# Latent attention in sets of four heads with 32-row scores, and the first two weight pieces together

## The chip, the cores and the metric

The kernel runs on one core of a Trainium2 chip. The metric is the device time in microseconds of one execution; the median of three runs of the kernel before is 1009.23 us (1008.88 to 1009.68). A matmul on this core multiplies a stationary operand (up to 128 rows by 128 columns, loaded by its own instruction) with a moving one of up to 512 columns and writes to a PSUM bank. There are eight banks of 128 partitions x 512 float32.

## The reference, cut to what matters

The model is a stack of two equal layers on x of 512 tokens by 1024 channels, float32, with a last RMSNorm. Each layer normalises x, projects it with w_in to three mixer branches and their gates, runs the branches (A: banded attention with sinks, B: gated linear attention, C: latent attention), projects each back, merges them by sigmoid gates, multiplies by w_out and adds x. The change touches branch C and the order of the first projections:

```
q_c = (rmsnorm(cq, cq_g) @ w_uq).reshape(B, S, 8, 64 + 32)        # q_nope, q_rope per head
kv  = (rmsnorm(ckv, ckv_g) @ w_ukv).reshape(B, S, 8, 64 + 64)     # k_nope, v per head
k_rope = rope(kr)                                                 # 32 numbers, shared by the heads
for each block of 128 queries:
    s = (q_nope @ k_nope.T + q_rope @ k_rope.T) * 96 ** -0.5
    s = where(key_chunk <= query_chunk, s, -1e30)                 # chunks of 64 tokens
    p = softmax(s);  y = p @ v
yc = y * silu(gc);  zc = yc @ w_oc
```

So query block 0 sees up to 128 keys, block 3 up to 512.

## The kernel before

**Pieces and quarters.** All weights come as 77 pieces of 128 x 1024 a layer. SP loads a piece into one of three buffers (`raw`). ScalarE rounds it to the high part `w_hi` (L793), VectorE makes the low part `w_lo` (L1095), and TensorE multiplies each tile three times (high x high, low x high, high x low; L569). TensorE takes a piece in four quarters; a quarter of a gate piece is six matmuls of 512 columns, and a piece's output lands in one of three ring banks, `ring0` to `ring2`. A buffer of `w_hi` is free when its piece is done, so ScalarE splits piece p + 3 right behind the last quarter of p, and VectorE its low part behind the second quarter of p + 1.

**What sets the order.** `make_schedule` writes one list of steps. Every engine walks through the same list in order and does its own part of each step, with semaphores between them. An engine that waits therefore holds back everything of its own that stands later in the list. `quarters(n)` takes n quarters of the fill, the gate pieces of branch C (53 to 64, 48 quarters), and adds a tanh (ScalarE, L951) after each piece and, for the first four, a silu (VectorE).

**The latent projections.** Piece 46 (`PUKV`) has eight outputs of 512 columns, four of v (even) and four of k (odd); pieces 47 and 48 (`PUQ`) have three each, the first two of them the rotary parts of q. An output of k or q holds two heads of 64 rows: ScalarE copies the upper 64 partitions (L865, L871), VectorE the lower ones (L1470, L1490), so that `k_c` and `q_c` hold every head in partitions 0 to 63, with the rotary parts in 64 to 95, brought by DMA through DRAM from ScalarE's queue.

**The latent attention.** There are 32 steps a layer, one for a head and a query block. `score_c` is one matmul of 96 rows by 128 columns against n = 128 to 512 keys into bank `nat[i % 2]` (L740). VectorE masks (L1350), takes the row maximum (L1352) and scales it (L1355); ScalarE makes the exponentials with their sum (L1014); VectorE takes the reciprocal (L1373) and multiplies (L1375, step `divide`). `turn` transposes the probabilities in blocks of 128 into the one bank `nat[2]` (L750), ScalarE copies them out (L1026), and `value_c` multiplies them with v for two heads at a time into `nat[3]`, 64 columns each (L777). Behind each eighth step `gate_branch` multiplies by the gate (L1114); `y_hi` and `y_lo` split the result. The steps are staggered: a turn is two steps behind its score, and one quarter stands between two steps.

**The start.** x comes as eight tiles. SP sends tile 0, half of piece 0, tile 1, its other half, tiles 2 to 7, then pieces 1 and 2. ScalarE and VectorE split the tiles as they come, TensorE does piece 0 tile by tile, then pieces 1 and 2. Then comes the sum of squares (`rms`, L641) and piece 3.

Of the kernel before, what the change touches and what calls it, by code (L numbers as in the profile page):

```python
# [66 lines left out]

def by_act(r):

    return sum(first_output(p) + o < r for p in (PUKV, PUQ, PUQ + 1) for o in range(outputs_of(p)) if act_reads(p, o))  # L70


def shared(p, o):

    return (p == PUKV and o % 2 == 1) or (p, o) == (PUQ, 2) or p == PUQ + 1


def act_reads(p, o):

    return p == PUKV or shared(p, o)  # L80


def by_dve(r):

    return r - sum(first_output(PUKV) + o < r for o in range(0, 8, 2))


def emptied_by(r):

    for p in (PUKV, PUQ, PUQ + 1):  # L90
        o = r - first_output(p)
        if 0 <= o < outputs_of(p):
            return not act_reads(p, o) or shared(p, o), act_reads(p, o)
    return True, False
# [17 lines left out]
def make_schedule():  # L112
# [85 lines left out]
    def quarters(n):  # L198

        for _ in range(min(n, len(fill))):  # L200
# [3 lines left out]
            if q % 4 == 3 and g is not None:  # L204
                b, j = g
                todo.append(("tanh", 12 * b + j))
                if 1 <= j <= BR:
                    todo.append(("silu", BR * b + j - 1))

# [26 lines left out]
    nc_ = TT * C_HEADS  # L236
    quarters(10)
    for i in range(nc_ + 3):
        if 2 <= i < nc_ + 2:
            todo.append(("turn", na + i - 2))  # L240
        if 1 <= i <= nc_:
            todo.append(("divide", na + i - 1))
        if i < nc_:
            todo.append(("score_c", i))
        if i >= 4 and i % 2 == 0:
            todo.append(("value_c", (i - 4) // 2))
        quarters(1)
        y, h = divmod(i - 3 + 1, C_HEADS)
        if y >= 1 and h < 2:
            todo.append((("y_hi", "y_lo")[h], TT + y - 1))  # L250
# [34 lines left out]
def build_hybrid_trunk(nc, x_t, pieces, params, alpha, tables, consts, final_g, out_t, k_rope_dram, q_rope_dram):  # L285
    with ExitStack() as ctx:
# [3 lines left out]
        def sig(name, per_layer, before=0):  # L290
# [39 lines left out]
        prob, prob_t = [work[:, i, :] for i in range(3)], [work[:, 3 + i, :] for i in range(4)]  # L330

# [3 lines left out]
        k_c = bank_g[:, :].rearrange("p (h n) -> p h n", h=C_HEADS)  # L335
# [5 lines left out]
        q_c = bank_a[:, 0:4096].rearrange("p (h n) -> p h n", h=C_HEADS)  # L341
# [20 lines left out]
        nat = [ctx.enter_context(nc.psum_tensor(f"nat{i}", [P, S], F32)) for i in range(4)]  # L362
        aux = ctx.enter_context(nc.psum_tensor("aux", [P, S], F32))
        turn_bank, o_bank = nat[2], nat[3]
# [7 lines left out]
        first_loaded, first_hi, first_lo = sig("first_loaded", 0), sig("first_hi", 0), sig("first_lo", 0)  # L372
# [23 lines left out]
        k_rope_saved, k_rope_placed = sig("k_rope_saved", 16), sig("k_rope_placed", 16)  # L396
        q_rope_saved, q_rope_placed = sig("q_rope_saved", 32), sig("q_rope_placed", 32)
# [12 lines left out]
        masked = sig("masked", A_KV + TT * C_HEADS)  # L410
        top_set = sig("top_set", 2 * TT * A_KV + TT * C_HEADS)
        neg_top_set, exp_done = sig("neg_top_set", n_steps), sig("exp_done", n_steps)
        turn_done, turn_out, value_done = (sig("turn_done", n_steps), sig("turn_out", n_steps),
                                           sig("value_done", TT * A_KV + TT * C_HEADS // 2))
        denom_set, divided = sig("denom_set", 2 * TT * A_KV + TT * C_HEADS), sig("divided", n_steps)
# [14 lines left out]
        def attention_of(step):  # L430

            if step < TT * A_KV:
                return "a", step // A_KV, step % A_KV, step // A_KV
            c = step - TT * A_KV
            return "c", c // C_HEADS, c % C_HEADS, TT + c // C_HEADS
# [7 lines left out]
        def _(sp):  # L443
            for j in range(KT):
                sp.dma_start(xt[:, j, :], x_t[:, j, :]).then_inc(x_loaded[j].sem, 16)  # L445
                if j == 0:
                    sp.dma_start(raw[:, 0, 0:512], pieces[0, :, 0:512]).then_inc(first_loaded.sem, 16)
                elif j == 1:
                    sp.dma_start(raw[:, 0, 512:1024], pieces[0, :, 512:1024]).then_inc(raw_loaded[0].sem, 16)
            for i in range(1, RAW):  # L450
                sp.dma_start(raw[:, i, :], pieces[i]).then_inc(raw_loaded[i].sem, 16)
# [4 lines left out]
            for n in range(RAW, DEPTH * PIECES):  # L456
                layer, p = divmod(n - RAW, PIECES)
                if p in (PQA[1] + 3, PQA[3] + 3):
# [3 lines left out]
                    for hh in range(GROUP):  # L462
                        for half in range(2):
                            sp.dma_start(q_a[64 * pair + 32 * half:64 * pair + 32 * half + 32, hh, :],
                                         work[32 * hh:32 * hh + 32, 4 + half, :]).then_inc(q_placed.sem, 16)
                sp.wait_ge(lo_split.sem, n - RAW + 1)
# [19 lines left out]
        def _(pe):  # L486
            def project(layer, quarter):
# [4 lines left out]
                if (layer, p, part) == (0, 0, 0):  # L492
                    pe.wait_ge(first_lo.sem, 1)
                elif part == 0 or (layer, p, part) == (0, 0, 2):
# [80 lines left out]
            def last_pieces():  # L575

                layer = DEPTH - 1
                for m in range(4):
# [9 lines left out]
                    for k in range(KT):  # L588
# [4 lines left out]
                        if (m, k) == (2, 5):  # L593
                            pe.wait_ge(aux_free.sem, aux_free.at(DEPTH, 0))
# [19 lines left out]

            def aux_bank(layer, u):
# [10 lines left out]
            for layer in range(DEPTH):  # L626
                u = 0
                for name, i in SCHEDULE:
                    if name == "quarter" and layer == DEPTH - 1 and i // 4 >= PIECES - 2:
                        if i == 4 * (PIECES - 2):  # L630
                            last_pieces()
                        continue
                    if name == "quarter":
                        project(layer, i)
                        continue
                    if (name, i) == ("rms", 0):

                        aux_bank(layer, u)
                        pe.wait_ge(setup_loaded.sem, SETUP)
# [91 lines left out]
                    elif name == "score_c":  # L731
                        qt, h = divmod(i, C_HEADS)
# [883 lines left out]
```

## Time and profile before

| | |
|---|---|
| median of three runs | 1009.23 us |
| the profiled execution | 1008.85 us, its span 1007.0 us |
| TensorE matmuls | busy 992.1 us (99%), 5168 instructions |
| VectorE | busy 624.7 us (62%) |
| ScalarE | busy 427.3 us (42%) |
| chain that ended last | TensorE 91%, ScalarE 3%, VectorE 3% |
| granted TensorE clock | 0.997 of full |
| latent attention in the chain | scores L740 3%, transposes L750 3%, values L777 2% |

Matmuls are pipelined: a record of a matmul is longer than its distance to the next one. What a matmul costs is read from the chain of waits, whose pieces stand end to end. An fp32 matmul (scores, values) shows as two instructions, a transpose as one, and each of the three products of L569 as one.

### The profile page before, as it was taken

What the parts mean: (1) busy time and instruction counts of PE and PEld (TensorE: products, weight loads), DVE (VectorE), ACT (ScalarE), POOL (GpSimd) and SP (SyncE); (2) the same over time, 40 slices, a digit from 0 to 9 for tenths busy, and PEclk for the clock granted to TensorE, in tenths of its full rate; (3) what the DMA queues carried; (4) which work ended last, traced back from release to release, by engine and by line L of the source; (5) the groups of instructions that cost most, each with busy time, mean ns of one, the idle gap of its engine ahead of it and who ended that gap; (6) DMA issues with size and microseconds to landing.
All of it is one profiled execution on the core that took longest, in us unless ns stands there. A gap on an engine that the chain in (4) does not pass through costs nothing.

```text
span 1007.0 us, 13335 instructions
## 1 busy us (share of the span) xinstructions
PE 992.1 (99%) x5168; PEld 792.8 (79%) x5168; DVE 624.7 (62%) x1142; ACT 427.3 (42%) x804; POOL 1.6 (0%) x6
## 2 busy tenths in 40 slices
PE   8999999999999999999999999999999999999996
PEld 6878878887777877788888887888877787767885
DVE  7746448546647576666556655584575667765844
ACT  6343335425542355533435333542354424554323
POOL 0000000000000000000000000000000000000000
PEclk9999999999999999999999999999999999999998
DMA  7323311322135211022223332122221522111212
GB/s 261 124 70 132 125 64 65 123 86 84 64 105 146 84 63 62 37 75 101 95 77 118 105 119 84 67 101 105 84 79 69 154 102 80 43 49 58 96 51 84
DMA packets 29952, 92.93 MB, mean 92 GB/s; under 512 B 3825, under 2 KB 6129, under 8 KB 29762
## 3 DMA queue, kind: packets, MB, share of 16 engines
q1 hardware_dynamic: 27362, 88.07, 24.7%
q10 hardware_dynamic: 2528, 4.02, 1.6%
q8 instruction: 41, 0.67, 0.3%
q14 instruction: 21, 0.17, 0.1%
HBM read 86.24 MB, written 3.28 MB: 89 GB/s over the span
## 4 chain that ended last, share of the span: by engine, by line
PE 91%; ACT 3%; DVE 3%; issue 1%; DMA 1%; SPq 0%; POOLq 0%; POOL 0%; ACTq 0%; DVEq 0%
PE ring L569 72%; PE nat L569 5%; PE nat L740 3%; PE nat L750 3%; PE nat L777 2%; ACT w_hi L793 1%; PE nat L763 1%; PE nat L703 1%; PE nat L726 1%; DVE w_lo L1095 1%; DMA raw<-pieces 1%; PE nat L691 0%; ACT gates L1042 0%; SPq L445 0%; PE aux L665 0%
## 5 line engine op out<-in xcount | busy, mean ns | idle before, releaser
L569 PE MATMUL ring<-act_hi,w_hi 128*128 128x512 f32 x848 | 348.8, 411 | 1.1 <-DVE w_lo L1095 0.9
L569 PE MATMUL ring<-act_hi,w_lo 128*128 128x512 f32 x848 | 331.1, 390 | 0.0
L569 PE MATMUL ring<-act_lo,w_hi 128*128 128x512 f32 x848 | 330.9, 390 | 0.0
L793 ACT ACTIVATE w_hi<-raw 128x1024 fp32r<-128x1024 f32 x153 | 161.5, 1057 | 340.2 <-PE ring L569 308.7
L1095 DVE TENSOR_TENSOR w_lo<-raw,w_hi 128x1024 fp32r<-128x1024 f32 x153 | 186.4, 1219 | 54.2 <-ACT w_hi L793 54.1
L569 PEld LDWEIGHTS ring<-act_hi,w_hi 128*128 128x128 f32 x848 | 159.3, 188 | 45.8 <-issue 11.8
L569 PEld LDWEIGHTS ring<-act_hi,w_lo 128*128 128x128 f32 x848 | 159.2, 188 | 34.4
L569 PEld LDWEIGHTS ring<-act_lo,w_hi 128*128 128x128 f32 x848 | 159.5, 188 | 32.6 <-issue 1.9
L1402 DVE SCALAR_TENSOR_TENSOR gates<-ring,rstd 128x512 f32<-128x512 f32 x72 | 49.7, 690 | 115.8 <-PE ring L569 115.2
L569 PE MATMUL ring<-y_hi,w_hi 128*128 128x512 f32 x192 | 74.8, 390 | 0.4 <-DVE bank_a L1490 0.4
L569 PE MATMUL ring<-y_hi,w_lo 128*128 128x512 f32 x192 | 74.7, 389 | 0.0
L569 PE MATMUL ring<-y_lo,w_hi 128*128 128x512 f32 x192 | 74.7, 389 | 0.0
L1014 ACT ACTIVATE work<-nat,neg_top 128x128 f32<-128x128 f32 (+3 forms) x64 | 33.8, 528 | 67.4 <-DVE neg_top L1355 67.2
L1026 ACT ACTIVATE work<-nat 128x512 f32<-128x512 f32 (+3 forms) x80 | 37.1, 463 | 32.7 <-PE nat L750 32.3
L569 PE MATMUL nat<-w_hi,act_hi 128*128 128x512 f32 (+1 forms) x128 | 49.1, 383 | 0.5 <-DVE w_lo L1095 0.5
L569 PE MATMUL nat<-w_lo,act_hi 128*128 128x512 f32 (+1 forms) x128 | 47.8, 374 | 0.0
L569 PE MATMUL nat<-w_hi,act_lo 128*128 128x512 f32 (+1 forms) x128 | 47.8, 373 | 0.0
L740 PE MATMUL nat<-bank_g,bank_a 96*128 96x128 f32 (+3 forms) x128 | 45.1, 433 | 0.0
L951 ACT ACTIVATE gates<-gates 128x512 f32<-128x512 f32 x72 | 43.6, 618 | 0.0
L569 PEld LDWEIGHTS ring<-y_hi,w_hi 128*128 128x128 f32 x192 | 36.0, 188 | 8.7 <-issue 1.2
L569 PEld LDWEIGHTS ring<-y_hi,w_lo 128*128 128x128 f32 x192 | 36.0, 188 | 7.5
L569 PEld LDWEIGHTS ring<-y_lo,w_hi 128*128 128x128 f32 x192 | 36.0, 188 | 7.4
(193 smaller groups left out, 1041.3 us busy)
## 6 DMA issues: line engine op xcount, KB each, us to landing
raw<-pieces SPq DMA_DIRECT2D x153, 512.0 KB, 3.5
xt<-x_t SPq DMA_DIRECT2D x8, 256.0 KB, 6.0
bank_a<-work SPq DMA_DIRECT2D x32, 64.0 KB, 2.0
out_t<-gates SPq DMA_DIRECT2D x7, 256.0 KB, 2.3
rope<-tables SPq DMA_DIRECT2D x1, 1024.0 KB
bank_g<-k_rope_dram ACTq DMA_DIRECT2D x2, 512.0 KB, 4.2
q_rope_dram<-work ACTq DMA_DIRECT2D x4, 256.0 KB, 2.2
bank_a<-q_rope_dram ACTq DMA_DIRECT2D x4, 256.0 KB, 6.2
```

Source lines behind the costliest of these rows:

```text
L569: mm = pe.matmul(dst, stationary, moving, start=start and i == 0, stop=stop and i == 2)
L703: mm = pe.matmul(nat[2 * pair + h][:, cs], state[half, c, pair, :], q_b[half, pair, cs], start=True, stop=True)
L726: mm = pe.matmul(nat[g][c * 64:c * 64 + 64, hh * P + skip:(hh + 1) * P], q_a[rows, hh, q0:q0 + CHUNK], k_a[rows, k0:q0 + CHUNK], start=Tru ...
L740: mm = pe.matmul(nat[i % 2][:, 0:n], q_c[0:C_DH, h, qt * P:(qt + 1) * P], k_c[0:C_DH, h, 0:n], start=True, stop=True)
L750: mm = pe.transpose(turn_bank[:, b * P:(b + 1) * P], prob[i % 3][:, b * P:(b + 1) * P], ident)
L777: mm = pe.matmul(o_t[r * 64:r * 64 + 64, f, :], v_c[:, b, h * C_V:(h + 1) * C_V], prob_t[(step + r) % 4][:, b * P:(b + 1) * P], start=b == ...
L793: nc.scalar.activation(w_hi[:, n % HL, :], raw[:, n % RAW, :], ACT.Copy).then_inc(hi_split.sem, 1)
L951: nc.scalar.activation(gates[:, j if j >= 4 else 8 + j, :], gates[:, j, :], ACT.Tanh).then_inc(gate_tanh.sem, 1)
L1014: nc.scalar.activation(prob[step % 3][:, 0:n], nat[i % 2][:, 0:n], ACT.Exp, scale=C_SCALE, bias=neg_top[:, step % 2, 0:1], accum_out=sums[ ...
L1026: nc.scalar.activation(prob_t[i % 4][:, 0:n], turn_bank[:, 0:n], ACT.Copy).then_inc(turn_out.sem, 1)
L1095: nc.vector.tensor_tensor(w_lo[:, n % HL, :], raw[:, n % RAW, :], w_hi[:, n % HL, :].bitcast(F32), ALU.subtract).then_inc(lo_split.sem, 1)
L1402: nc.vector.scalar_tensor_tensor(gates[:, j, :], res, 0.5, rstd[:, :], ALU.mult, ALU.mult).then_inc(proj_free.sem, 1)
```

## The change

Four things change.

1. **Scores in sets of four heads.** The rows of k and q are laid out so that head a of a set (a = 0 to 3) sits in partitions 32a to 32a + 31, in three parts: two halves of the 64 unrotated rows (`q_n`, `k_n`) and the rotary 32 (`q_r`, `k_r`). A score is three matmuls of 32 rows that add up in one bank; the four heads go to the four banks `nat[0]` to `nat[3]`. There are 8 sets a layer, 12 matmuls each. Transposes go back into the bank that the head's scores came from, and the values of a set are one group. The values' output moves to bank `aux`. VectorE masks four heads and reduces two at a time.
2. **Projections.** An output of v, and each of q, is emptied by ScalarE alone, one of k by VectorE alone, 128 partitions at a time. The rotary parts of k go by 4 DMAs of SP, ahead of the load of piece 52, those of q by 16, ahead of the load of piece 55.
3. **The order of the steps.** A set is: score, values of the set before, a quarter, divide, a quarter, `y_hi` of a finished query block, 1, 1, 2 or 3 quarters (by query block), `y_lo`, transposes, a quarter.
4. **The start.** The first halves of pieces 0 and 1 come behind tiles 0 and 1, their second halves behind tiles 3 and 4; TensorE does both pieces together, into two ring banks.

TensorE in the first layer, third query block (384 keys), before. L750 are transposes, L740 a score, L777 values, L569 the fill:

```order
1526 L750 MATMUL nat<-con,work 128x128 x3
1527 L740 MATMUL nat<-bank_g,bank_a 128x384
1528 L777 MATMUL nat<-work,bank_a 64x128 x4
1529 L569 MATMUL ring<-act_hi,w_hi 128x512
1530 L569 MATMUL ring<-act_lo,w_hi 128x512
```

The same place now, the sixth set (L782 transposes, L775 scores, L818 values, L575 the fill):

```order
1506 L782 MATMUL nat<-con,work 128x128 x12
1507 L575 MATMUL ring<-act_hi,w_hi 128x512
1508 L575 MATMUL ring<-act_lo,w_hi 128x512
1509 L575 MATMUL ring<-act_hi,w_lo 128x512
1510 L575 MATMUL ring<-act_hi,w_hi 128x512
1511 L575 MATMUL ring<-act_lo,w_hi 128x512
1512 L575 MATMUL ring<-act_hi,w_lo 128x512
1513 L775 MATMUL nat<-bank_g,bank_a 128x384 x12
1514 L818 MATMUL aux<-work,bank_a 64x128 x7
```

One transpose group, score and value group stand for four heads, and the score comes a quarter behind the transposes of the set before it, whose copies it waits for.

ScalarE in the same query block, before. L1014 is an exponential, L1026 a copy of transposes, L793 a weight split, L951 a tanh:

```order
472 L1014 ACTIVATE work,sums<-nat,neg_top 128x384
473 L793 ACTIVATE w_hi<-raw 128x1024
474 L951 ACTIVATE gates<-gates 128x512
475 L1026 ACTIVATE work<-nat 128x384
476 L1014 ACTIVATE work,sums<-nat,neg_top 128x384
```

ScalarE now, the fifth set and the start of the sixth (L1037 exponentials, L1058 `y_hi`, L834 weight split, L971 tanh, L1050 copies):

```order
386 L1037 ACTIVATE work,sums<-nat,neg_top 128x384 x4
387 L1058 ACTIVATE y_hi<-y_pre 128x4x128
388 L834 ACTIVATE w_hi<-raw 128x1024
389 L971 ACTIVATE gates<-gates 128x512
390 L1050 ACTIVATE work<-nat 128x384 x3
391 L1050 ACTIVATE bank_a<-nat 128x384
392 L1037 ACTIVATE work,sums<-nat,neg_top 128x384 x4
```

Four copies in a row now stand behind the split and the tanh of a piece that ends right before the transposes.

SP at the start, before (x_t is x, pieces the weights):

```order
1 L445 DMA xt<-x_t 128x512
2 L447 DMA raw<-pieces 128x512
3 L445 DMA xt<-x_t 128x512
4 L449 DMA raw<-pieces 128x512
5 L445 DMA xt<-x_t 128x512 x6
6 L451 DMA raw<-pieces 128x1024 x2
```

SP at the start now:

```order
1 L442 DMA xt<-x_t 128x512
2 L444 DMA raw<-pieces 128x512
3 L442 DMA xt<-x_t 128x512
4 L444 DMA raw<-pieces 128x512
5 L442 DMA xt<-x_t 128x512 x2
6 L446 DMA raw<-pieces 128x512
7 L442 DMA xt<-x_t 128x512
8 L446 DMA raw<-pieces 128x512
9 L442 DMA xt<-x_t 128x512 x3
10 L447 DMA raw<-pieces 128x1024
```

Piece 1 moved ahead of the last tiles of x, in two halves.

The core of the diff:

```diff
+    for y in range(2 * TT):
+        qt = y // 2
+        todo.append(("score_c", y))
+        if y > 0:
+            todo.append(("value_c", y - 1))
         quarters(1)
+        todo.append(("divide_c", y))
+        quarters(1)
+        if y > 0 and y % 2 == 0:
+            todo.append(("y_hi", TT + qt - 1))
+        quarters((1, 1, 2, 3)[qt])
+        if y > 0 and y % 2 == 0:
+            todo.append(("y_lo", TT + qt - 1))
+        todo.append(("turn_c", y))
+        quarters(1)
...
-        mm = pe.matmul(nat[i % 2][:, 0:n], q_c[0:C_DH, h, qt * P:(qt + 1) * P],
-                       k_c[0:C_DH, h, 0:n], start=True, stop=True)
+        pe.wait_ge(turn_out.sem, turn_out.at(layer, NA + 4 * i))
+        for part in range(3):
+            for a in range(4):
+                rows = slice(32 * a, 32 * a + 32)
+                q, k = ((q_n[rows, g, part, ts], k_n[rows, g, part, 0:n]) if part < 2 else
+                        (q_r[rows, g, ts], k_r[rows, 0:n]))
+                mm = pe.matmul(nat[a][:, 0:n], q, k, start=part == 0, stop=part == 2)
...
+    elif name == "turn_c":                                   # ScalarE
+        act.wait_ge(value_done.sem, value_done.at(layer, NA + i))
+        for a in range(4):
+            act.wait_ge(turn_done.sem, turn_done.at(layer, NA + 4 * i + a + 1))
+            nc.scalar.activation(prob_ct[a][:, 0:n], nat[a][:, 0:n], ACT.Copy).then_inc(turn_out.sem, 1)
...
+    for k in range(2):                                       # VectorE, divide_c
+        h = 4 * g + 2 * k
+        dve.wait_ge(exp_done.sem, exp_done.at(layer, NA + 4 * i + 2 * k + 2))
+        nc.vector.reciprocal(recip[:, h:h + 2], sums[:, qt, h:h + 2]).then_inc(denom_set.sem, 1)
...
+    elif p == PUQ + 5:                                       # SP
+        sp.wait_ge(rope_out.sem, rope_out.at(layer, 10))
+        for g, half, a in ((g, half, a) for g in range(2) for half in range(2) for a in range(GROUP)):
+            sp.dma_start(q_r[32 * a + 16 * half:32 * a + 16 * half + 16, g, :],
+                         work[64 * g + 16 * a:64 * g + 16 * a + 16, 2 * half, :]).then_inc(q_rope_placed.sem, 16)
...
-    for o in ((2,) if p == PUQ else range(3)):               # VectorE
-        nc.vector.tensor_copy(q_c[0:64, h, :], ring[(first_output(p) + o) % 3][0:64, :])
...
+def first_pieces():                                          # TensorE
+    jobs = [(p, k) for p in range(2) for k in range(2)] + [(p, k) for k in range(2, KT) for p in range(2)]
```

## Rows read from the trace of the kernel before

**Rows 1.** The page: engine busy time, and shares of the chain.

```profile
PE 992.1 (99%) x5168; PEld 792.8 (79%) x5168; DVE 624.7 (62%) x1142; ACT 427.3 (42%) x804; POOL 1.6 (0%) x6
PE 91%; ACT 3%; DVE 3%; issue 1%; DMA 1%; SPq 0%; POOLq 0%; POOL 0%; ACTq 0%; DVEq 0%
```

**Rows 2.** Chain of waits, first layer's latent attention: start us, us, what.

```profile
343.26 0.22 PE nat L740 x2
...
409.38 0.44 PE nat L750 x4
409.82 0.86 PE nat L740 x2
410.68 1.38 PE ring L569 x6
...
413.35 1.02 PE nat L777 x16
414.38 1.58 PE ring L569 x6
...
431.14 0.89 PE ring L569 x3
```

**Rows 3.** Timeline of TensorE: start us, us, instruction; one banded score group.

```profile
238.38 1.10 PE L726 MATMUL nat<-bank_a 64*64 64x128 f32 x32
```

**Rows 4.** Chain of waits, first layer's gated linear attention.

```profile
130.89 0.60 PE nat L691 x16
...
139.87 1.04 PE nat L703 x16
```

**Rows 5.** Groups of weight loads by line: busy us, mean ns of one.

```profile
L740 PEld LDWEIGHTS nat<-bank_g,bank_a 96*128 96x128 f32 x128 | 19.7, 191 | 1.4
...
L691 PEld LDWEIGHTS nat<-bank_g 64*64 64x64 f32 x128 | 3.4, 132 | 2.8 <-issue 2.8
```

**Rows 6.** Groups by line and form on ScalarE and VectorE.

```profile
L1014 ACT ACTIVATION_READ_ACCUMULATOR work<-nat,neg_top 128x1 f32 x64 | 12.4, 193 | 0.0
...
L1352 DVE TENSOR_REDUCE top<-nat 128x1 f32<-128x512 f32 x16 | 11.1, 691 | 0.5
...
L1014 ACT ACTIVATE work<-nat,neg_top 128x512 f32<-128x512 f32 x16 | 11.0, 688 | 18.2 <-DVE neg_top L1355 18.2
...
L1026 ACT ACTIVATE work<-nat 128x384 f32<-128x384 f32 x16 | 7.8, 488 | 4.4 <-PE nat L750 4.0
L1375 DVE TENSOR_SCALAR work<-work,recip 128x512 f32<-128x512 f32 x16 | 7.8, 486 | 0.6
```

**Rows 7.** Chain of waits at the third step of the latent attention.

```profile
345.08 1.39 PE ring L569 x6
...
348.14 0.17 ACT work L1026
...
348.44 0.30 PE nat L750
```

**Rows 8.** Timeline of TensorE, latent projections and first output projection.

```profile
305.26 0.39 PE L569 MATMUL ring<-lat_hi,w_lo 128*128 128x512 f32 x1
305.79 0.47 PE L569 MATMUL ring<-lat_hi,w_hi 128*128 128x512 f32 x1
...
307.02 0.39 PE L569 MATMUL ring<-lat_hi,w_lo 128*128 128x512 f32 x1
307.63 0.47 PE L569 MATMUL ring<-y_hi,w_hi 128*128 128x512 f32 x1 [0.22 <-DVE bank_a L1490]
```

**Rows 9.** Timeline at the start, TensorE and VectorE.

```profile
15.24 0.50 PE L569 MATMUL ring<-act_hi,w_hi 128*128 128x512 f32 x1 [0.91 <-DVE w_lo L1095]
...
24.33 2.28 DVE L1095 TENSOR_TENSOR w_lo<-raw,w_hi 128x1024 fp32r<-128x1024 f32 x2
...
26.30 1.02 PE L641 MATMUL aux<-merged,ones_r 128*128 128x512 f32 x2
```

**Rows 10.** SP's queue: rotary parts of the banded queries.

```profile
73.19 6.05 SPq L464 DMA_DIRECT2D bank_a<-work  x8
```

More of the change, by code:

```diff
@@ L65, in first_output, with act_reads @@
     return sum(outputs_of(q) for q in range(p))
+def act_reads(p, o):
+    return (p == PUKV and o % 2 == 0) or (p, o) == (PUQ, 2) or p == PUQ + 1
 def by_act(r):
     return sum(first_output(p) + o < r for p in (PUKV, PUQ, PUQ + 1) for o in range(outputs_of(p)) if act_reads(p, o))
[L73 to L80, printed above, removed]
 def by_dve(r):
-    return r - sum(first_output(PUKV) + o < r for o in range(0, 8, 2))
+    return r - by_act(r)
 def emptied_by(r):
[L90 to L94, printed above, removed]
+    by_scalar = by_act(r + 1) > by_act(r)
+    return not by_scalar, by_scalar
 def signals_before(p):
@@ L206, in quarters @@
                 todo.append(("tanh", 12 * b + j))
-                if 1 <= j <= BR:
+                if 1 <= j <= BR and (b, j) != (2, BR):
                     todo.append(("silu", BR * b + j - 1))
+                if (b, j) == (2, BR - 1):
+                    todo.append(("silu", BR * b + j))
     fill = [4 * p + q for p in [*range(PO[0], PO[0] + 4), *range(PG[1], PG[1] + 12)] for q in range(4)]
@@ L235, in make_schedule @@
     fill = [4 * p + q for p in range(PG[2], PG[2] + 12) for q in range(4)]
[L236 to L246, printed above, removed]
-        quarters(1)
-        y, h = divmod(i - 3 + 1, C_HEADS)
-        if y >= 1 and h < 2:
-            todo.append((("y_hi", "y_lo")[h], TT + y - 1))
+    quarters(8)
+    for y in range(2 * TT):
[3 more added lines that the diff above has]
+            todo.append(("value_c", y - 1))
+        quarters(1)
+        todo.append(("divide_c", y))
[7 more added lines that the diff above has]
+        quarters(1)
+    todo.append(("value_c", 2 * TT - 1))
+    quarters(1)
+    todo.append(("y_hi", 2 * TT - 1))
     quarters(len(fill) - 1)
@@ L330, in build_hybrid_trunk @@
         prob, prob_t = [work[:, i, :] for i in range(3)], [work[:, 3 + i, :] for i in range(4)]
+        prob_c, prob_ct = [work[:, i, :] for i in range(4)], [*(work[:, 4 + i, :] for i in range(3)), bank_a[:, 3072:3584]]
         k_dec = bank_g[:, 0:1024].rearrange("p (t n) -> p t n", t=TT)
@@ L632, in _ @@
                         continue
+                    if name == "quarter" and layer == 0 and i // 4 < 2:
+                        if i == 0:
+                            first_pieces()
+                        continue
                     if name == "quarter":
@@ L748, in _ @@
                             pe.wait_ge(turn_out.sem, turn_out.at(layer, i))
-                        for b in range(GROUP if kind == "a" else qt + 1):
+                        for b in range(GROUP):
                             mm = pe.transpose(turn_bank[:, b * P:(b + 1) * P], prob[i % 3][:, b * P:(b + 1) * P], ident)
```

339 lines of the change are left out of this document (170 added, 169 removed).

## The prediction, made before the changed kernel ran

> **What bounds the kernel now.** The page comes first: TensorE is busy for 992.1 of 1007.0 us and makes up 91% of the chain that ended last [rows 1]. So an edit counts by what it does to TensorE's stream, and by the few gaps in it. Then the chain of waits inside the first layer's latent attention, from the first score to the last value group, 343.26 to 431.14 us [rows 2]: it is an unbroken row of TensorE pieces, a score matmul being two instructions (0.22 us at 128 keys, 0.86 at 512, so 0.43 and 0.65 between), a transpose 0.11, a value group of 16 instructions 1.02, a fill quarter of six matmuls 1.38, or 1.58 behind a value group. ScalarE and VectorE are hidden there but for one gap near 348 us [rows 7]. The second layer repeats it. Last come the start [rows 9] and the latent projections [rows 8], where TensorE does wait.
>
> **Scores.** Before, 32 matmuls a layer, 8 for each query block: 8 x (0.22 + 0.43 + 0.65 + 0.86) = 17.3 us. After, a set of four heads is 12 matmuls of 32 rows, 24 instructions, and there are 8 sets. An instruction streams as long as before, so a set costs 24 half-prices over the number of row groups that really work side by side. No row shows four row groups. The nearest by kind is the banded score L726: 32 instructions of 64 rows x 64 columns, four tiles at a time (two row groups by two column groups), took 1.10 us where one behind the other they would take 32 x 0.108 = 3.5: less some 0.2 for the change of mode, that is four at a time [rows 3]. I take four: 6 half-prices, 0.65, 1.30, 1.94 and 2.59 us.
>
> The weight loads may set a floor. The state readout L703 loads 128 columns for every 64-column stream: 16 instructions took 1.04 us, less 0.17 of entry 0.054 each [rows 4]. At that rate 24 loads need 1.30 us, more than the 0.65 of a 128-key set. In the other direction, a 128-column load lasts 191 ns against 132 for 64 columns [rows 5], so a column costs 0.9 ns and 128 of them about 0.11 us; two row groups must then have loaded side by side in L703, and four could give 0.65 us per set. I take 1.30, the row of the same width. Four sets of 128 keys in all make 2.6 us between the ends.
>
> Sets of one layer: 2 x (1.30 + 1.30 + 1.94 + 2.59) = 14.3 us, 3.0 less than before, **6.0 for both layers**. The ends: 8.6 if loads run four abreast; below, if row groups overlap less, the rivals.
>
> **Changes of mode.** A value group of 16 costs 1.02 - 16 x 0.054 = 0.16 us to enter, and the quarter behind it is 0.20 longer than one behind a score [rows 2]. Before: 16 groups a layer, 5.8 us. After: 8 entries into the 32-row mode at 0.17 (L691: 0.60 - 16 x 0.027 [rows 4]), 8 into the value mode, 9 ways back: 1.36 + 1.28 + 1.80 = 4.4. **Saved 1.3 a layer, 2.6 in all.** If the way between the two small modes were free or double, that is 1.1 us for each layer to either side. Transposes and values stay at 80 x 0.11 and 160 x 0.054.
>
> **Waits inside a set.** All four banks now hold one set from score to transpose, so between score and transposes stand only three to five quarters and the last value group. The longest chain, 512 keys: two reductions over a pair (about twice 0.69 each [rows 6]; the first pair is ready at 1.8 us behind the score, the second at 3.2), four exponentials at some 0.78 with the accumulator read (to 4.9), reciprocals and multiplications of 0.49 (to 6.3). Cover: five quarters and a value group, 8.5 us. At 384 keys 5.5 against 6.7; at 128 keys 3.7 against 4.3. VectorE's gate evacuation (0.69) and one silu stand ahead of the reductions, and are over as the first scores end. For the third set two silus stand there, the second behind its tanh; then the pairs are ready at 5.7 to 6.9 us after the quarter, and the transposes, one head after another, start at 6.4. Hidden, with little to spare.
>
> One wait isn't hidden. In the fifth set (384 keys) the transposes come right behind a piece's last quarter. On ScalarE that quarter's weight split and tanh then stand ahead of the four copies out of the banks; the next score waits for all four. The chain at 346 us shows how long: quarter over at 346.48, tanh through at 348.14 [rows 7]. So the copies start 1.75 us after the transposes begin, four of 0.49 (0.43 apart, since they overlap) end at 3.6; TensorE has 1.3 of transposes and one quarter, 2.7. **0.95 us lost a layer**; before lost about 0.4 near 348. Net +1.1 for both. With shorter copies this is 0; if the same happened in the third and sixth sets too, +4.
>
> **Latent projections.** k_c and q_c were emptied half by ScalarE, half by VectorE, each with 64 partitions and about the time that 128 take. Now one engine takes one output. VectorE's q copies stood behind six rotary operations and a weight split; TensorE waited for them: 305.26 + 0.23 to 305.79, and 307.02 + 0.23 to 307.63 [rows 8], 0.68 us. They go, since ScalarE is idle there. The earlier gaps hang on the first v copy and on the rotary multiplications and stay. **1.4 us for both layers** (0 to 3). The rotary parts go through 16 DMAs of SP ahead of piece 55's load. Eight of that kind took 6.05 us to issue [rows 10], so 16 about 12 us, from 310 to 322 us. The load is then some 6 us late, but its split is due only near 329 and the first score near 340.
>
> **Start.** TensorE waits 0.91 us ahead of piece 1, which starts at 15.24; pieces 1 and 2 end at 26.30 [rows 9]. Three pieces are 72 x 0.227 = 16.3 us and could start at about 8.2: 24.6. With both pieces fed by each tile of x, a tile gives 1.36 us of work and the splits take 0.7 to 1.4, so TensorE stays fed. But piece 3 needs its low part, which VectorE starts at 24.33 behind the squares and has at 25.5. TensorE would want it at about 25.1 after the mean square; before, the mean square started at 26.30 and piece 3 at about 27.1. **1.6 us** (0.5 if the tiles moved back in the queue arrive late, 2.2 if VectorE gets ahead too).
>
> **Sum.** 6.0 + 2.6 - 1.1 + 1.4 + 1.6 = 10.5 us. The profiled execution took 1008.85 us, so 998.35; the median of the runs is 0.4 higher: **998.7 us**. About 0.2% (2 us) is what a measurement of this kernel can tell from no change.
>
> **Rivals.**
> A. Row groups overlap threefold only, by a shared path into or out of the array. For it: in L726 only two row groups ran at a time. Against it: there the factor was whole. Price: sets of 1.30, 1.73, 2.59 and 3.45 us, 18.1 a layer instead of 14.3, +7.7: 1006.4 us. Beside this: the Trainium skill, "TensorE: Matmul & The Clock Gate", in "Measured speedup vs the span model", gives 3.07-fold for four row tiles of K=32 and N=512; by that figure the time would be an estimated 1006 us. No row here shows four row groups, and the L726 row points the other way.
> B. Row groups go in pairs, since each stream of four writes all 128 partitions of its own bank. This is the slower case. Its place is every set. For it: L703, the only row with 128-column outputs from two row groups, took 0.87 us net for sixteen streams of 0.054, which is also what no overlap at all would give [rows 4]. Against it: L691 and L726. Price at two abreast: 12 half-prices, 1.30, 2.59, 3.89, 5.18: 25.9 a layer, 11.6 more than my sum: 998.7 + 23 = 1022 us. It decides below about 2.6 abreast; there the sets eat up the other gains. With no overlap, 24 half-prices, 51.8 a layer: 1074 us.
> C. The sets' chain is too long for its cover, as four banks leave no second set in flight. For it: the chain at 346 us shows ScalarE's queue reaching TensorE. Against it: the covers worked out above. At 1 us in each of the first four sets of a layer: +8, 1006.7 us.
> D. Loads go four abreast and the copies of the fifth set are in time: 998.7 - 2.6 - 1.9 = 994.2 us.
>
> **How the numbers follow.** My forecast 0.55, D 0.15, A 0.1, C 0.07, B 0.1 with both its forms, other 0.03. The range 994 to 1007 takes in D, A and C and leaves out B. Faster holds the forecast, D, A and most of C: 0.84. Within 0.2%: 0.05, from the edge of A and C. Slower: 0.11.
>
> **What would show it.** In the new chain, 24 score instructions at 512 keys in about 2.6 us (3.5 speaks for A, 5.2 for B), at 128 keys 1.3 (0.65 for D). A wait for ScalarE's copies of about 1 us ahead of the sixth set's score, in both layers, and none of size at the other sets. No VectorE wait near 305 and 307. The start of piece 3 near 25.5 us. Matmul starts within a set that stand one stream apart instead of four at once would make the forecast wrong.

## The result and the profile after

The changed kernel took 994.08 us (median of 4 runs, 993.81 to 994.21) against 1009.45 us before (1008.88 to 1009.75): ratio 0.9849, 95% interval 0.9837 to 0.9861, 15.4 us faster. The forecast was 998.7 us, with 994.0 to 1007.0 as the range. The direction was right, and so was the mechanism, four row groups abreast. The time came out almost exactly where rival D put it (994.2 us). D's ground, weight loads four abreast, is what the trace shows; that the number agrees so closely is in part luck, as the part on the prediction works out.

The page after, engine busy time [rows 1]:

```profile
PE 978.3 (99%) x5424; PEld 791.6 (80%) x5424; DVE 600.6 (61%) x991; ACT 417.8 (42%) x797; POOL 1.6 (0%) x6
```

TensorE is as full as before and has 13.8 us less to do; it still sets the time. The chain of waits of the changed kernel through the first layer's latent attention (start us, us, what) answers to [rows 2]:

```profile
338.04 0.88 PE nat L775 x24
...
343.25 0.44 PE nat L782 x4
343.69 1.38 PE ring L575 x6
...
345.95 0.59 PE aux L818 x8
346.54 4.33 PE ring L575 x18
...
352.70 1.51 PE nat L775 x24
...
372.63 1.02 PE aux L818 x16
373.65 5.68 PE ring L575 x24
...
379.42 0.69 ACT w_hi L834
...
380.38 0.31 ACT gates L971
...
380.90 1.23 ACT work L1050 x3
382.13 0.39 ACT bank_a L1050
...
394.61 2.79 PE nat L775 x24
...
405.91 1.75 PE nat L782 x16
...
411.83 1.90 PE aux L818 x32
...
425.78 2.26 PE ring L575 x9
```

Every L775 piece is one set of four heads: 24 instructions in 0.88, 1.51, 2.15 to 2.22 and 2.79 us for 128, 256, 384 and 512 keys. Less 0.23 of entry that is 0.65, 1.28, 1.92 to 1.99 and 2.56: six times the half of a matmul before (0.108, 0.216, 0.323, 0.43), at every length. Four row groups really run abreast, and so do their weight loads. A group of values (L818) costs 0.16 beside its matmuls, and the quarters behind one 0.19 more (4.33 against 3 x 1.38). Transposes (L782) cost 0.11 each and next to nothing at their borders: a quarter behind them takes 1.38 to 1.40, where six matmuls in an unbroken stretch take 6 x 0.227 = 1.36. The values of the last set end at 425.78.

The one wait is where it was forecast: behind the fifth set's transposes ScalarE has a weight split and a gate ahead of the four copies, and the sixth set's scores wait for the last copy. The timeline of TensorE there (the row holds 20 of the set's 24 instructions):

```profile
382.56 1.90 PE L775 MATMUL nat<-bank_g,bank_a 32*128 32x384 f32 x20 [0.55 <-ACT bank_a L1050]
```

In the latent projections the two VectorE waits of [rows 8] are gone; the chain is one row of TensorE from 292.93 us on, with a gap of 0.11 us in it:

```profile
292.93 8.01 PE ring L575 x33
300.93 0.11 issue
301.04 11.16 PE ring L575 x48
```

At the start, piece 3 comes at 26.08 us, still behind VectorE's low part. Piece 3 was forecast for 25.5; the low part begins at 24.88, 0.55 us later than in [rows 9], where I had left it:

```profile
24.88 2.28 DVE L1118 TENSOR_TENSOR w_lo<-raw,w_hi 128x1024 fp32r<-128x1024 f32 x2
...
26.08 0.46 PE L575 MATMUL nat<-w_hi,act_hi 128*128 128x432 f32 x1 [0.74 <-DVE w_lo L1118]
```

The kernel before has one more wait for VectorE's low part a little later, which is gone now:

```profile
42.11 0.47 PE L569 MATMUL nat<-w_hi,act_hi 128*128 128x432 f32 x1 [0.26 <-DVE w_lo L1095]
```

SP's sixteen rotary transfers took 10.00 us to issue, from 308.65 us, and nothing waited for them, as forecast from [rows 10]:

```profile
308.65 10.00 SPq L472 DMA_DIRECT2D bank_a<-work  x16
```

The span fell by 15.0 us (1007.0 to 992.0). By stages: TensorE reaches the first expansion 1.56 us earlier; from there to the next branch each layer is 0.83 shorter (15.52 to 14.69); the stage of the latent attention, from there to the first matmul of the branch's own output projection, 5.7 shorter in the first layer (129.02 to 123.3) and about the same in the second; about 0.4 is left over at the end. 1.56 + 2 x 0.83 + 2 x 5.7 + 0.4 = 15.0. The stage begins and ends with these matmuls now (before, 307.63 [rows 8] and 436.65):

```profile
305.24 0.39 PE L575 MATMUL ring<-y_hi,w_hi 128*128 128x512 f32 x1
...
428.56 0.39 PE L575 MATMUL ring<-y_hi,w_hi 128*128 128x512 f32 x1
```

### The profile page after: what moved, and what is told of

It is laid out like the page before. It is cut to its first block, busy times and chain, and to the rows that moved or that the text cites. A ratio compares the mean times of both kernels' runs of the same rounds, so it can differ in the third digit from the quotient of the medians.

```text
span 992.0 us, 13563 instructions
## 1 busy us (share of the span) xinstructions
PE 978.3 (99%) x5424; PEld 791.6 (80%) x5424; DVE 600.6 (61%) x991; ACT 417.8 (42%) x797; POOL 1.6 (0%) x6
## 4 chain that ended last, share of the span: by engine, by line
PE 92%; ACT 3%; DVE 2%; issue 1%; DMA 1%; SPq 1%; POOLq 0%; POOL 0%; ACTq 0%; DVEq 0%
PE ring L575 72%; PE nat L575 7%; PE nat L775 3%; PE aux L818 2%; PE nat L782 1%; PE aux L804 1%; PE nat L790 1%; PE nat L732 1%; PE nat L755 1%; DMA raw<-pieces 1%; ACT w_hi L834 1%; PE nat L720 0%; DVE w_lo L1118 0%; SPq L442 0%; ACT gates L1065 0%
## 5 line engine op out<-in xcount | busy, mean ns | idle before, releaser
L575 PE MATMUL ring<-act_hi,w_hi 128*128 128x512 f32 x832 | 333.5, 401 | 0.0
L575 PE MATMUL ring<-act_hi,w_lo 128*128 128x512 f32 x832 | 325.1, 391 | 0.0
L575 PE MATMUL ring<-act_lo,w_hi 128*128 128x512 f32 x832 | 324.7, 390 | 0.0
L834 ACT ACTIVATE w_hi<-raw 128x1024 fp32r<-128x1024 f32 x152 | 160.5, 1058 | 352.2 <-PE ring L575 320.4
L575 PEld LDWEIGHTS ring<-act_hi,w_hi 128*128 128x128 f32 x832 | 156.3, 188 | 37.8 <-issue 7.2
L575 PEld LDWEIGHTS ring<-act_hi,w_lo 128*128 128x128 f32 x832 | 156.2, 188 | 33.6
L575 PEld LDWEIGHTS ring<-act_lo,w_hi 128*128 128x128 f32 x832 | 156.5, 188 | 30.1
L575 PE MATMUL ring<-y_hi,w_lo 128*128 128x512 f32 x192 | 74.8, 389 | 0.0
L575 PE MATMUL ring<-y_hi,w_hi 128*128 128x512 f32 x192 | 74.8, 389 | 0.0
L575 PE MATMUL ring<-y_lo,w_hi 128*128 128x512 f32 x192 | 74.8, 389 | 0.0
L575 PE MATMUL nat<-w_hi,act_hi 128*128 128x512 f32 (+1 forms) x128 | 48.7, 381 | 1.0 <-DVE w_lo L1118 1.0
L1037 ACT ACTIVATE work<-nat,neg_top 128x128 f32<-128x128 f32 (+3 forms) x64 | 32.9, 526 | 38.7 <-DVE neg_top L1380 38.7
L575 PE MATMUL nat<-w_lo,act_hi 128*128 128x512 f32 (+1 forms) x128 | 47.9, 374 | 0.0
L575 PE MATMUL nat<-w_hi,act_lo 128*128 128x512 f32 (+1 forms) x128 | 47.8, 374 | 0.0
L971 ACT ACTIVATE gates<-gates 128x512 f32<-128x512 f32 x72 | 43.6, 618 | 1.7 <-DVE gates L1431 1.6
L575 PEld LDWEIGHTS ring<-y_hi,w_lo 128*128 128x128 f32 x192 | 36.1, 188 | 7.5
L575 PEld LDWEIGHTS ring<-y_lo,w_hi 128*128 128x128 f32 x192 | 36.1, 188 | 7.5
L575 PEld LDWEIGHTS ring<-y_hi,w_hi 128*128 128x128 f32 x192 | 36.1, 188 | 7.4
L775 PE MATMUL nat<-bank_g,bank_a 32*128 32x128 f32 (+3 forms) x384 | 30.4, 446 | 1.1 <-ACT bank_a L1050 1.1
L1481 DVE SCALAR_TENSOR_TENSOR gates<-gates,ring 128x512 f32<-128x512 f32 x32 | 22.0, 687 | 14.8 <-PE ring L575 14.8
```

The source lines that it names most:

```text
L575: mm = pe.matmul(dst, stationary, moving, start=start and i == 0, stop=stop and i == 2)
L775: mm = pe.matmul(nat[a][:, 0:n], q, k, start=part == 0, stop=part == 2)
L834: nc.scalar.activation(w_hi[:, n % HL, :], raw[:, n % RAW, :], ACT.Copy).then_inc(hi_split.sem, 1)
L971: nc.scalar.activation(gates[:, j if j >= 4 else 8 + j, :], gates[:, j, :], ACT.Tanh).then_inc(gate_tanh.sem, 1)
L1037: nc.scalar.activation(prob_c[a][:, 0:n], nat[a][:, 0:n], ACT.Exp, scale=C_SCALE, bias=neg_top[:, i % 2, a:a + 1], accum_out=sums[:, qt, 4 ...
L1481: nc.vector.scalar_tensor_tensor(merged[:, j, :] if b == 0 else tile, tile, 1.0, z, ALU.add, ALU.mult).then_inc(proj_free.sem, 1)
```

## The experiments

Medians are of runs beside runs of the kernel before on the same chip; the ratio is to that kernel, with its 95% interval. The changed kernel was run again as the measure: 994.24 us (993.95 to 994.67), 0.9850 (0.9836 to 0.9863). The runs stand on three chips, on which the kernel before took 1009.39, 1009.27 and 1009.29 us, so their times can be set beside each other.

> The changed kernel unchanged, as the measure for the others on the same chip: 994.1 us, ratio to before 0.985. Every theory expects that.

**Two small parts undone.** First the start of before:

```
-            def first_pieces():  (both pieces, tile by tile)
+            project(layer, i) for pieces 0 and 1, piece 0 loaded in halves, piece 1 behind the tiles of x
```

> The start of before with the rest of the change. In the two traces TensorE comes to the second latent projection's expansion 1.56 us earlier after the change (290.55 against 292.11 us). If that is all that the new start brings, and nothing later takes it back, this kernel is 1.4 to 1.8 us slower than the changed one (about 995.7). If TensorE would later have stood at a transfer anyway, the difference is under 0.5 us.

Measured 995.97 us (995.54 to 996.03), 0.9866 (0.9853 to 0.9880): 1.7 us slower than the changed kernel. The intervals of the ratios overlap, the runs themselves do not. The new start is worth what its stage shows, and nothing takes it back. Both waits of the old start, 0.9 us at piece 1 and 0.26 near 42 us, are back in its trace.

Then the emptying of the query accumulators:

```
-    return (p == PUKV and o % 2 == 0) or (p, o) == (PUQ, 2) or p == PUQ + 1
+    return p == PUKV and o % 2 == 0          (VectorE copies the four others)
```

> VectorE alone empties the query accumulators that the change gave to ScalarE (one of the second query piece's outputs and the three of the last). In before TensorE stood there four times, near 305.3 to 307.6 us, and the stretch from the first expansion to the next branch fell from 15.52 to 14.69 us per layer, 0.83. Theory: the sharing of the emptying between two engines is what removed these waits, so here 0.5 to 0.8 us per layer come back, 1.0 to 1.6 us in all (about 995.4). Rival: the shorter stretch comes from two accumulators and their copies of 64 rows that are gone altogether, and who empties the rest is of no account: under 0.3 us.

Measured 995.45 us, 0.9861 (0.9847 to 0.9874), 1.2 us slower. The intervals of the two kernels overlap, so the trace has to carry it. Its chain of waits:

```profile
303.02 0.61 DVE bank_a L1515
303.63 0.04 issue
303.67 1.65 PE ring L575 x6
```

VectorE's rotary operations and its copy are back in the chain ahead of TensorE. From the first expansion to the first score this kernel takes 45.84 us (292.52 to 338.36) and the changed one 45.09 (292.79 to 337.88): 0.75 per layer. The sharing is what removed the waits.

**The price of a border.** The values in two groups with a quarter between:

```
-            todo.append(("value_c", y - 1))
+            todo.append(("value_h", y - 1))      first half
         quarters(1)
+            todo.append(("value_c", y - 1))      second half
```

> The values of each set stand in two groups with a quarter of a projection between them, instead of in one; the matmuls are the same. Theory: a way into the values' tiles and back out of them has a price of its own, about 0.16 us in (a group of 8 values takes 0.59 us, of 16 1.02, of 24 1.46, of 32 1.90) and 0.19 us back (three quarters take 4.33 us behind such a group, 3 x 1.38 = 4.14 elsewhere). Seven more groups in each layer make 7 x 0.35 = 2.5 us, about 5 us in all (999). Rival: the price belongs to something else, as the first use of a copied matrix, and the number of groups is of no account: under 1 us.

Measured 999.25 us, 0.9904 (0.9888 to 0.9921), 5.0 us slower, as forecast. The chain shows each half-group with its own entry and its own long quarter:

```profile
345.69 0.37 PE aux L823 x4
346.06 1.60 PE ring L578 x6
347.66 0.37 PE aux L823 x4
348.03 2.95 PE ring L578 x12
```

A group of 4 takes 0.37, that is 0.16 + 4 x 0.054, and the quarter behind it 1.60 where 1.39 is usual. 5.0 us over 14 groups (the halves of the last set have no quarter between them) is 0.36 for each: the border price is real and additive.

**The wait at the fifth set.** One quarter moved:

```
-        quarters((1, 1, 2, 3)[qt])
+        quarters((1, 1, 1, 1, 3, 2, 2, 3)[y])
```

> One quarter of a projection is moved from before the transposes of the fifth set to before those of the seventh or eighth (1, 1, 1, 1, 3, 2, 2, 3 quarters at that place instead of 1, 1, 1, 1, 2, 2, 3, 3), so that no piece of 128 columns ends just before a set's transposes. In the changed kernel TensorE stands 0.53 us at the fifth set, since ScalarE splits a weight piece (1.06 us) and takes a gate (0.61 us) before it copies the four transposed matrices. Theory: the order of these on ScalarE is the cause, and the wait goes: 0.4 to 0.6 us per layer, about 1.0 us in all (993.1). Rival: the wait moves to the seventh or eighth set, where a piece then ends at the same place and a set has four blocks: no difference, or up to 1 us slower.

Measured 993.03 us, 0.9838 (0.9824 to 0.9851), and 992.75, 0.9834 (0.9820 to 0.9847), in a second measurement on another chip:

> The kernel with the moved quarter once more, as the measure for the wide sets on the same chip: 993.0 us.

The chain has no ScalarE in it any more, and nothing new stands at the later sets:

```profile
373.36 7.03 PE ring L575 x30
380.39 1.31 PE nat L782 x12
381.70 1.39 PE ring L575 x6
383.08 2.15 PE nat L775 x24
```

From the first score to the last value it is 87.14 us, against 87.74 in the changed kernel: 0.6 per layer. Each difference in time is within what the intervals allow, but both runs and the trace agree.

**The cover of the chain.** In the sets of 384 and 512 keys one quarter between scores and transposes, instead of four and five:

```
         todo.append(("divide_c", y))
-        quarters(1)
+        quarters((1, 1, 0, 0)[qt])
...
-        quarters((1, 1, 2, 3)[qt])
+        quarters((1, 1, 0, 0)[qt])
```

> In the sets of 384 and 512 keys only one quarter of a projection stands between a set's scores (and the values of the set before) and its transposes, instead of four and five; the quarters left over stand behind the last set. In the changed kernel the chain from the end of the scores to the last multiplication takes 5.6 us at 384 keys (384.78 to about 390.4) and 5.9 us at 512 (411.83 to about 417.7). With one quarter the last head's transposes would come 2.3 to 3.0 us after the scores at 384 keys and 4.4 to 4.8 us at 512 before any wait (1.02 or 1.46 us of values at 384, 1.46 or 1.90 at 512, 0.19 + 1.38 of the quarter, three of the four transposes of 0.33 or 0.44 each). Theory: TensorE stands for the rest, and nothing gives it back: about 2.1, 1.6, 1.5 and 1.1 us, 6.3 per layer, 12.6 in all (1007; 1003 to 1010). That is the price of the chain where its cover is gone. Rival: the chain is short since its engines were late for other work only, and shrinks with the quarters: under 4 us.

Measured 1005.91 us, 0.9967 (0.9955 to 0.9979), 11.7 us slower; forecast 12.6. The transposes of the four sets end 1.7, 1.2, 1.7 and 1.3 us later than without a wait, 5.9 a layer where 6.3 was worked out. Only part of this shows as idle time of TensorE, since the transposes of a group also come further apart (us in total, times, longest):

```profile
PE nat L782 <- DVE work L1404: 9.5, 12, 1.5
```

So the chain that rival C feared is about as long as worked out, and only the fill hides it. In the changed kernel it is hidden at all eight sets. The eighth set, on VectorE and then ScalarE:

```profile
412.06 0.27 DVE L1373 MEMSET nat<- 64x256 f32 x1 [2.29 <-PE nat L775]
...
416.85 0.88 DVE L1404 TENSOR_SCALAR work<-work,recip 128x512 f32<-128x512 f32 x2
```

```profile
413.84 0.69 ACT L1037 ACTIVATE work<-nat,neg_top 128x512 f32<-128x512 f32 x1 [3.12 <-DVE neg_top L1380]
```

The scores end at 411.83, the last multiplication at 417.73 (5.9 us), and the transposes begin at 420.76.

**How four row groups come to run abreast.** Only the order of the twelve matmuls of a set was changed, in three ways. Two heads in turn:

```
-                        for part in range(3):
-                            for a in range(4):
+                        for part, a in [(part, a) for pair in ((0, 1), (2, 3)) for part in range(3) for a in pair]:
```

> The same 24 instructions of a score set with only two heads in turn: heads 0 and 1 first, then 2 and 3, so that two row groups are abreast. Theory: the time of a set goes by its stream: 12 prices of half a matmul and 0.23 us of entry instead of 6, so 1.5, 2.8, 4.1 and 5.4 us for a set of 128, 256, 384 and 512 keys instead of 0.88, 1.51, 2.2 and 2.79: 2 x (0.65 + 1.29 + 1.94 + 2.58) = 12.9 us more per layer, 25.9 in all (1020). Rival: weight loads go one after another, whatever the row group, and matmuls of 128 keys are bound by them: then the sets of 128 and 256 keys grow by less, and the sum is under 22 us.

Measured 1004.19 us, 0.9949 (0.9930 to 0.9969): 10.0 us slower, not 26. Head by head:

```
-                        for part in range(3):
-                            for a in range(4):
+                        for a in range(4):
+                            for part in range(3):
```

> The same 24 instructions of a score set, but the three matmuls of one head (one group of 32 rows, one bank) stand one behind the other instead of one of each head in turn. Theory 1: TensorE starts instructions in their order, and only neighbours of different row groups run beside each other. Then a set has hardly more than one or two abreast: up to 24 prices of half a matmul (0.108, 0.216, 0.323, 0.43 us at 128, 256, 384, 512 keys) instead of 6, and 18 more of them per set are 2 x 18 x (0.108 + 0.216 + 0.323 + 0.43) = 39 us per layer, 78 us in all; with one neighbour abreast at each change of the head (24 less 3 x 1) 66 us. Theory 2: each row group has a queue of its own, deep enough for six instructions, and they are drained beside each other: no difference.

Measured 1025.01 us, 1.0156 (1.0135 to 1.0176): 30.8 us slower, neither 0 nor 66 to 78. Both my theories of it were wrong. In pairs the theory was wrong on the size; the sum that its rival allowed (under 22 us) holds, but not its ground, since the sets of 512 keys took 3.75 us and not 5.4. The sets of pairs took 1.20, 2.04, 2.90 to 2.97 and 3.75 us, the head by head ones 1.85, 3.11, 4.39 to 4.46 and 5.67. Less entry, 512 keys are 8.2 and 12.6 half-prices. What happened is seen when a 512-key set is cut into stretches of 0.432 us, one half-price each; the count behind "PE busy" is of the matmul instructions that run in the stretch, some of them counted in two. Two heads in turn:

```profile
397.47:397.90 0.43, 0.43 (x2) 0.29 (x4) 1.00 0.72 257
397.90:398.33 0.43, 0.43 (x4) 0.19 (x2) 1.00 0.95 371
398.33:398.77 0.44, 0.44 (x6) 0.31 (x6) 1.00 1.04 428
398.77:399.20 0.43, 0.43 (x8) 0.31 (x4) 1.00 0.39 153
...
400.06:400.49 0.43, 0.43 (x6) 0.19 (x2) 1.00 0.00 0
400.49:400.93 0.44, 0.44 (x4) 0.00 (x0) 1.00 0.00 0
```

Two half-prices with one pair alone, then both pairs together, then the second pair alone: 2 + 6 = 8. Head by head the count climbs by one in a stretch:

```profile
403.86:404.29 0.43, 0.43 (x1) 0.29 (x2) 1.00 0.50 76
404.29:404.72 0.43, 0.43 (x2) 0.18 (x1) 1.00 0.72 295
404.72:405.16 0.44, 0.44 (x3) 0.29 (x3) 1.00 1.06 438
```

In the changed kernel it is 4 and then 8 at once:

```profile
394.38:394.81 0.43, 0.43 (x4) 0.31 (x8) 1.00 0.74 200
394.81:395.24 0.43, 0.43 (x8) 0.20 (x4) 1.00 1.01 410
```

Both odd results follow if a row group takes four half-instructions, one that runs and three behind it, before it holds up what follows for other row groups. A head has six. In pairs the fifth and sixth of heads 0 and 1 get in after one and two half-prices, so heads 2 and 3 start at two and end at 8. Head by head, each starts two later than the one before: 6 + 3 x 2 = 12. Since this was made to fit two numbers, it was put to a third order:

```
+                        for part, a in [(part, a) for parts in ((0, 1), (2,)) for a in range(4) for part in parts]:
```

> The order of a score set's 24 instructions between the changed kernel's and the head by head one: both matmuls of the unrotated rows of head 0, then of head 1, 2 and 3, and then the rotated rows' matmul of each head. The two runs with other orders gave 8 half-matmul prices for two heads in turn (3.75 us at 512 keys, less 0.23 of entry, by 0.43) and 12.6 for head by head (5.67), where neighbours alone abreast would give 12 and over 20. In both, a row group that comes later begins two half-prices after the six instructions of the one before it. Theory: a row group takes up to four instructions ahead (one that runs and three that stand behind it), and only the fifth holds back all that follow, on whatever row group. Then four of each row group go in at once here, and a set takes 6 half-prices as in the changed kernel: 2.79 us at 512 keys, 994.2 in all (within 1 us). Rival: what counts is how far apart two row groups' first instructions stand (here 4 instead of 2 places), or the instructions ahead in all, some 8: then a set takes 8 to 9 half-prices, 3.7 us at 512 keys, about 1004.

Measured 994.43 us, 0.9850 (0.9837 to 0.9864), the same as the changed kernel, with sets of 2.81 us at 512 keys. The rival, a limit on the instructions ahead in all, would have given some 1004. Four per row group is thus borne out: with three, this order would take 9 half-prices, and with five the head by head order would take 9 as well, since head 1 would start after one. I also worked the orders through with a bound on all instructions ahead together in place of one for each row group, and no number fits: six give 12 head by head, but 11 in pairs, and the 13 that this third order would need give 7 in pairs and 8 head by head. Whether a row group holds four half-instructions or two whole matmuls, these orders can't tell.

Four heads' scores in one bank, instead of one bank each, were not tried.

**A faster version.** With the border prices known (0.23 + 0.16 + 0.19 for a set) the two sets of 128 keys were joined to one of eight heads, and the two of 256 keys too, on top of the moved quarter:

```
+    sets = [0, 2, 4, 5, 6, 7]
...
+        quarters({0: 5, 2: 5, 4: 3, 5: 2, 6: 2, 7: 3}[y])
...
+                        for j, part, a in [(j, part, a) for j in members(i) for part in range(3) for a in range(4)]:
+                                mm = pe.matmul(nat[a][:, cols], q, k, start=part == 0, stop=part == 2)
```

> On top of the moved quarter (993.0 us): the two sets of 128 keys are made one set of all eight heads (the second four in the next 128 columns of the same banks), and so are the two of 256 keys; six sets in a layer instead of eight, the same matmuls. Theory: what a group costs beside its matmuls is a fixed price at its border, 0.23 us into the scores, 0.16 into the values and 0.19 back, and each set that is gone saves 0.58: two in each layer, four in all, 2.3 us (990.7). The chain of the wide set of 256 keys (four reductions, eight exponentials of about 0.45 us) is some 6.5 us and stands behind six quarters, 8.3 us and more, so no wait takes its place. Rival: the eight exponentials and the copies of two sets at a time come late, or collide with a weight piece's split on ScalarE, and take back 0.5 to 2 us: 991 to 993.

Measured 989.88 us (989.84 to 990.16), 0.9807 (0.9793 to 0.9820), beside 992.75 of the moved quarter alone on the same chip: 2.9 us, forecast 2.3; the stages of the two traces give 2.6 of it. Against the changed kernel it is 0.4% faster, with intervals that don't overlap. Its chain:

```profile
337.87 1.55 PE nat L788 x48
339.42 9.75 PE ring L587 x42
...
351.44 2.80 PE nat L788 x48
354.24 1.02 PE aux L834 x16
```

48 instructions take 1.55 where two sets took 2 x 0.88, and 42 projection matmuls run on without a border. Per layer the attention is 85.85 us instead of 87.14, so 1.3: scores 0.43, values 0.30, ways back 0.57. The rival, a wait in place of the borders, shows nowhere in the chain.

## Why the prediction was right, and where its sizes were off

**Scores**, forecast 6.0 with ends of 8.6. The step "I take four" was right. With their entries the scores fell from 17.3 to 14.7 us a layer, 2.55; the forecast had 3.0 less 1.36 of entries, 1.64. The mis-sized term is the load floor: "At that rate 24 loads need 1.30 us ... I take 1.30, the row of the same width". They needed 0.65. The groups of weight loads in the changed kernel (busy us, mean ns of one):

```profile
L775 PEld LDWEIGHTS nat<-bank_g,bank_a 32*128 32x128 f32 x384 | 16.7, 185 | 12.6 <-issue 8.6 <-ACT bank_a L1050 2.0
```

A load lasts 185 ns, as in [rows 5], but 24 of them fit into a set of 0.88. The bound from the other direction, two row groups loading side by side in L703 and four here, was the true one. What weighed against it was only that the other row had the same width; it had two row groups, and the number of row groups is what the sum turned on. That is 1.3 us a layer on paper; 0.9 of it shows in the comparison above, since each of the eight entries took 0.23 instead of 0.17.

**Changes of mode**, forecast 2.6 for both layers. By the chain, the value groups fell from 11.2 to 9.9 us a layer, and what the fill loses at its borders from 4.2 to 2.4. A quarter behind a small-tile group is 0.23 to 0.24 over the unbroken stretch, one behind a full score or a transpose 0.03; before there were 16 and 19 such borders a layer, now there are 9 and 8. The 19 small ones were not in the forecast. Less 8 entries of 0.23 into the scores, that is 1.2 a layer, 2.3 in all. The split values and the wide sets show the same prices by adding and by removing groups.

**Waits**, forecast +1.1. The place and the cause were right (the moved quarter removes it), the size was not: 0.53 a layer instead of 0.95. The copies began 1.57 us behind the start of the transposes instead of 1.75, and came 0.40 apart instead of 0.43. Before, the gap near 348 us cost 0.44 [rows 7]: the transpose at 348.44 began 0.25 late and took 0.30 instead of 0.11. So the term is +0.2 instead of +1.1 us.

**Latent projections**, forecast 1.4, measured 1.66 in the stages: right. How much of it hangs on who empties the accumulators is 1.2 us in time and 1.5 by the stages of the two traces.

**Start**, forecast 1.6, measured 1.56 by the stage and 1.7 by undoing it. The working was less good than the number. Piece 3 came only 1.0 us earlier (its second matmul at 27.36 before and 26.38 now), since VectorE's low part began 0.55 later than I took it to. Most of the rest was made up where the kernel before waits again for a low part, at 42.11 us; that wait was not in the forecast.

**Rivals.** A, threefold overlap, is excluded: 2.56 us for 24 half-prices of 0.432 is 4.0-fold, and 3.7-fold with the entry. The Trainium skill's 3.07 ("TensorE: Matmul & The Clock Gate", "Measured speedup vs the span model") does not hold for these matmuls. An order that fills the row groups less well gives less, two heads in turn 2.9-fold (10.4 over 3.52) and head by head 1.9-fold. B is excluded as the changed kernel stands, and the order head by head shows where it would have lain: at 1025 us the change is slower than before. C's chain exists and costs 11.7 us without its cover; the cover was counted rightly. D's assumptions were loads four abreast, which came out, and the fifth set's copies in time, which came out by half (a wait of 0.53 a layer instead of 0.95 or none). Against D's sum, the dearer entries cost 0.8 us and the waits 1.0; borders gave back 0.6, the projections 0.3 and the end 0.4, and some 0.5 is not accounted for. That these cancel to 0.1 us is luck.

**What stays open.** Scores 2.55, value groups 1.2 and the fill's borders 1.8, less 0.1 of waits, are 5.45 of the 5.7 us by which the stage became shorter in a layer; the other 0.25 is a remainder that no run isolates. The 0.4 at the end lies behind GpSimd's last instruction: from TensorE's last projection to there, 20 us, the two traces agree to 0.03, but the last output transfer then took 3.3 us before and 2.9 after. In the second trace of the changed kernel it took 2.5, with GpSimd's instruction 1.2 later. The same kernel thus differs from itself by as much there, and nothing says that the change is behind the 0.4.

## What to carry to other kernels

- A small-tile matmul that can run beside others is to be issued in turn over all row groups, with no more than two fp32 matmuls of one row group in a row. The same twelve matmuls of 512 keys cost 2.79 or 5.67 us by their order alone.
- Where no row shows an operation, take the row that is like it in the quantity on which the price hangs (here the number of row groups), not the one that looks alike; and keep the other end in the range.
- Each change between full and small tiles has a price of its own at either side, so few large groups beat many small ones, as long as the fill between covers the softmax chain.

## What the runs showed of the hardware

- Four row groups of 32 ran fully abreast for fp32 matmuls of 128 to 512 columns, each into its own bank: 24 instructions in 0.23 us + 6 x 0.432 at 512.
- Weight loads of different row groups run abreast too: 24 of 185 ns each beside the matmuls of a set of 0.88 us.
- A row group takes about four half-instructions (two fp32 matmuls) ahead; the next one holds up all that follow. Within that, a later instruction of another row group starts before an earlier one of a busy row group: 8.2 and 12.6 half-prices for two other orders, 6 for a third.
- Border prices, in us: 0.23 into the 32-row scores, 0.16 into the values of 64 columns; 0.23 to 0.24 back to the full fill, over an unbroken stretch of it. Behind a full score or a transpose the fill loses 0.03. 14 more value groups cost 5.0 us.
- ScalarE's exponentials of 512 columns with their sums came 0.67 us apart, its copies of 384 columns 0.40, each less than its own duration of 0.69 and 0.49.
